# A decoder layer with retrieval over 16384 experts: the last block's scores from one dense product, with v rows gathered alone

## The reference

```python
q = (xb @ wq).reshape(PEER_BLOCK, PEER_HEADS, 2, PEER_HALF)        # 8 heads
s = jnp.einsum('thpd,hpkd->thpk', q, subkeys)                      # 128 keys a side
sv, si = lax.top_k(s, PEER_TOPK)                                   # 16
cand, cand_id = ...                                                # 16 x 16 pairs of a head
top_v, top_i = lax.top_k(cand, PEER_TOPK)
expert = jnp.take_along_axis(cand_id, top_i, axis=-1)              # 8 x 16 = 128 a token
gate = softmax(top_v)
act = gelu(einsum('thkd,td->thk', u_tab[expert], xb))              # 128 dots of width 1024
out = einsum('thk,thkd->td', gate * act, v_tab[expert])
```

## Time and profile before

| | |
|---|---|
| runs | 4586.57, 4585.86, 4565.0 us; median 4585.86 |
| profiled execution, span from first to last instruction | 4574.9 us (its own time is not listed; the runs stand 10 us below to 12 us above the span) |
| TensorE | 3277.9 us busy, 72% |
| VectorE | 2488.2 us, 54% |
| GpSimd | 1648.0 us, 36% |
| ScalarE | 801.6 us, 18% |
| DMA | 1400.14 MB, mean 306 GB/s |

### The profile page before, as it was taken

How to read it: one execution, slowest core, us unless ns; L and a number is a source line. 1 busy time by engine, 2 the same in 40 slices (tenths; PEclk the granted TensorE clock), 3 DMA queues, 4 the chain that set the end, 5 groups by cost and what they waited for, 6 DMA issues and landing times. The chain is left out here.

```text
span 4574.9 us, 46652 instructions
## 1 busy us (share of the span) xinstructions
PE 3277.9 (72%) x15679; PEld 1680.7 (37%) x15679; DVE 2488.2 (54%) x7735; ACT 801.6 (18%) x1284; POOL 1648.0 (36%) x1379
## 2 busy tenths in 40 slices
PE   8899997736389666686678676667666667666666
PEld 2798896636056441341145344124210101111110
DVE  2245553126764445577755454557786555555554
ACT  2232333232014113110013211211000100000000
POOL 1211104523245444442345444344333333333332
PEclk9999998968589886897789888678765666666666
DMA  7211103533789889898889898999899999999998
GB/s 278 73 58 49 39 29 131 171 118 111 274 334 407 338 354 379 345 384 341 337 348 405 345 393 356 383 375 362 354 387 360 415 404 405 409 412 409 414 411 346
DMA packets 243430, 1400.14 MB, mean 306 GB/s; under 512 B 30661, under 2 KB 47685, under 8 KB 100986
## 3 DMA queue, kind: packets, MB, share of 16 engines
q0 software_dynamic: 156672, 1140.92, 62.1%
q1 hardware_dynamic: 86522, 256.22, 15.5%
HBM read 1345.59 MB, written 51.43 MB: 305 GB/s over the span
## 5 line engine op out<-in xcount | busy, mean ns | idle before, releaser
L1057 DVE CUSTOM_DVE_ANT_0 peer_uv<-peer_uv,all_PS 128x512 f32<-128x512 f32 x2176 | 1435.3, 685 | 1164.2 <-DMA peer_uv<-in_uv,peer_idx 804.8
L996 PE MATMUL all_PS<-peer_hT,peer_sel 96*128 96x512 bf16 x2176 | 1002.4, 484 | 1027.4 <-DVE peer_halves L1057 842.5
L979 POOL DMA_INDIRECT peer_uv<-in_uv,peer_idx x1088 | 1043.4, 959 | 1756.9 <-PE all_PS L1015 1379.6
L996 PEld LDWEIGHTS all_PS<-peer_hT,peer_sel 96*128 96x128 bf16 x2176 | 203.0, 102 | 2002.9 <-DVE peer_halves L1057 1632.6
L1015 PE MATMUL all_PS<-peer_uv,peer_zw 128*32 128x512 f32 x4352 | 871.7, 849 | 2.4 <-DVE peer_zw L1077 2.4
L867 POOL TENSOR_TENSOR flow_w_lo<-flow_w,flow_w_hi 128x1024 fp32r<-128x1024 f32 (+1 forms) x204 | 460.4, 2261 | 456.5 <-ACT flow_w_hi L860 455.9
L1031 ACT ACTIVATE peer_ge<-peer_pre 128x4 f32<-128x4 f32 x272 | 55.7, 205 | 2109.7 <-DVE peer_pre L1063 2109.6
L887 PE MATMUL all_PS<-mix_h_hi,flow_w_hi 128*128 128x384 f32 (+1 forms) x672 | 279.6, 416 | 32.2 <-POOL flow_w_lo L867 31.8
L860 ACT ACTIVATE flow_w_hi<-flow_w 128x1024 fp32r<-128x1024 f32 (+1 forms) x204 | 203.5, 1003 | 359.2 <-PE all_PS L889 110.7
L888 PE MATMUL all_PS<-mix_h_lo,flow_w_hi 128*128 128x384 f32 (+1 forms) x672 | 226.3, 337 | 0.0
L889 PE MATMUL all_PS<-mix_h_hi,flow_w_lo 128*128 128x384 f32 (+1 forms) x672 | 226.1, 336 | 0.0
(11 more groups left out here) (290 smaller groups left out, 4670.4 us busy)
## 6 DMA issues: line engine op xcount, KB each, us to landing
cond_w<-in_w_ada SPq DMA_DIRECT2D x12, 2048.0 KB, 8.1
flow_w<-in_w_gate_ab SPq DMA_DIRECT2D x48, 512.0 KB, 7.1
flow_w<-in_w_query SPq DMA_DIRECT2D x48, 512.0 KB, 7.7
flow_w<-in_w_conv SPq DMA_DIRECT2D x36, 512.0 KB, 4.5
peer_uv<-in_uv,peer_idx POOLq DMA_INDIRECT x1088, 10.4
gla_w<-in_w_heads SPq DMA_DIRECT2D x24, 512.0 KB, 4.4
flow_w<-in_w_proj_b SPq DMA_DIRECT2D x24, 512.0 KB, 7.8
flow_w<-in_w_out SPq DMA_DIRECT2D x24, 512.0 KB, 8.4
```

Of the source, the lines that this page charges most:

```text
L979: self.nc.gpsimd.indirect_dma_start(out=self.uv[:, n % self.NUV, :], out_offset=None, in_=self.A["uv"], in_offset=bass.IndirectOffsetOnAxi ...
L996: nc.tensor.matmul(PS[:, f, :], self.sel[:, c:c + 1].broadcast_to([3 * GR, P]), self.hT[:, g % self.NH, f * 512:(f + 1) * 512], start=True ...
L1057: nc.vector.tensor_tensor_reduce(part, part, PS[:, f, :], 1.0, 0.0, ALU.mult, ALU.add, self.halves[:, d, f, e:e + 1]).then_inc(M["dotted"], 1)
```

## The change

The last block (part 2, tiles 6, 7 and 8 in order, 384 tokens, `SCORED`) is treated in another way than the rest.

- In part 2's pick stage TensorE multiplies the tile's h with the whole table u^T, in 32 chunks of 512 experts, each in four steps of two slices of k, with the same three products. The table's blocks (`u_chunks`, 128 of 512 KB) go through the weight stream, halves included. `emptied` copies each chunk of scores from PSUM to `line`, and SyncE stores it in DRAM (`scores2`). h_hi and h_lo of the keys stage now live through pick.
- For a scored token `fetch` issues two indirect DMAs: the v row of each expert (4 KB, from the same table seen as 32768 rows) and one element of 4 bytes for each expert from the stored scores. There is no `spread` and no `dots`; `gelu` reads the fetched scores. `gat.limit` keeps scored tokens from being fetched before the last stage.
- The ring of buffers is 18 slots of 4 KB a partition (a whole row takes two), `AHEAD` is 12 where slots are free, and the stream has four raw buffers in place of two.
- `SHARES` is given for each part. A part without scored tiles ends at its last share: part 0 at 24 and part 1 at 100. Part 2 ends at token 704.
- norm makes no `pieces` for scored tiles. `make_low_on_vector` is called in all stages and applies to blocks in `by_vector`, which is empty here, because only a part behind a scored one fills it.

```diff
+SCORED = frozenset((6, 7, 8))
+CHUNK, KPAIR = 512, 2
+NCHUNK, NKP = NK * NK // CHUNK, KD // KPAIR
...
-    def __init__(self, sc, sources, raws=2, pairs=4):
-        self.sources, self.raws, self.pairs = sources, raws, pairs
+    def __init__(self, sc, sources, by_vector, raws=4, pairs=4):
+        self.sources, self.by_vector, self.raws, self.pairs = sources, by_vector, raws, pairs
...
-    NUV, NZ, ND, NH, AHEAD = 10, 3, 4, 6, 4
+    NUV, NZ, ND, NH, NS, AHEAD = 9, 3, 4, 6, 8, 12
+    NIDX = 6
...
     def fetch(self, pool, upto):
 
-        for n in self.steps("pool", upto + self.AHEAD if upto else 0):
+        end = min(upto, self.limit)
+        while upto and end < min(upto + self.AHEAD, self.limit) and self.freed[end] <= max(upto - 3, 0) // BT:
+            end += 1
+        for n in self.steps("pool", end):
             u, c, j = self.tokens[n]
+            q, e = divmod(n, BT)
             if n == self.before[u]:
                 pool.wait_ge(self.M["idx_set"], u + 1)
-            if n >= self.NUV:
-                pool.wait_ge(self.M["v_mm"], (n - self.NUV) // BT + 1)
...
+            if self.freed[n]:
+                pool.wait_ge(self.M["v_mm"], self.freed[n])
+            at, slot = j * GR + c, self.place[n]
+            index = lambda of: bass.IndirectOffsetOnAxis(ap=of[:, u % self.NIDX, at:at + 1], axis=0)
+            if not self.scored[n]:
+                self.nc.gpsimd.indirect_dma_start(out=self.uv[:, slot:slot + 2, :].rearrange("p s d -> p (s d)"), out_offset=None,
+                                                  in_=self.A["uv"], in_offset=index(self.idx)).then_inc(self.uv_in[slot], 16)
+                continue
+            s = self.scored_before[q]
+            if e == 0 and s >= self.NS:
+                pool.wait_ge(self.M["gelled"], q - self.NS + 1)
+            self.nc.gpsimd.indirect_dma_start(out=self.uv[:, slot, :], out_offset=None,
+                                              in_=self.A["uv"].rearrange("e (s d) -> (e s) d", s=2), in_offset=index(self.idx)
+                                              ).then_inc(self.uv_in[slot], 16)
+            self.nc.gpsimd.indirect_dma_start(out=self.score[:, s % self.NS, e:e + 1], out_offset=None,
+                                              in_=self.A[f"scores{self.part_of[u]}"].rearrange("d p (s o) -> (d p s) o", o=1), in_offset=index(self.spot)
+                                              ).then_inc(self.s_in[s % self.NS], 16)
...
         @block.tensor
         def _(pe):
-            for j in range(NJ):
-                gat.spread(pe, upto(j))
-                i, q = divmod(j, PARTS_OF)
+            def chunk(j):
+
+                c, k2 = divmod(j, NKP)
+                u_hi, u_lo = (a[:, (w0 + j) % w.pairs].rearrange("p (k f) e -> p k (f e)", k=KPAIR) for a in (w.hi, w.lo))
+                pe.wait_ge(w.low, w0 + j + 1)
+                for i, t in enumerate(scored):
+                    m = c * nd + i
+                    tok = slice(part.at[t], part.at[t] + P)
+                    if k2 == 0 and m >= 3:
+                        pe.wait_ge(l_out, m - 2)
+                    for kk in range(KPAIR):
+                        k = KPAIR * k2 + kk
+                        nc.tensor.matmul(bank(m), h_hi[:, k, tok], u_hi[:, kk, :], start=(k == 0), stop=False)
+                        nc.tensor.matmul(bank(m), h_hi[:, k, tok], u_lo[:, kk, :], start=False, stop=False)
+                        last = nc.tensor.matmul(bank(m), h_lo[:, k, tok], u_hi[:, kk, :], start=False, stop=(k == KD - 1))
+                        if k == KD - 1 and i < nd - 1:
+                            last.then_inc(c_mm, 1)
+                        if kk == KPAIR - 1 and i == nd - 1:
+                            last.then_inc(w.used, 1)
+                        gat.spread(pe, turns.within(j, KPAIR * i + kk + 1, KPAIR * nd))
...
+            def emptied(c):
+
+                for i in range(nd):
+                    m = c * nd + i
+                    if i < nd - 1:
+                        act.wait_ge(c_mm, c * (nd - 1) + i + 1)
+                    else:
+                        act.wait_ge(w.used, w0 + c * NKP + NKP)
+                    if m >= NR:
+                        act.wait_ge(l_saved[m % NR], 16 * (m // NR))
+                    nc.scalar.activation(line[:, m % NR, :], bank(m), ACT.Copy).then_inc(l_out, 1)
             for j in range(NJ):
                 gat.gelu(act, upto(j))
-                i, q = divmod(j, PARTS_OF)
+                if nd:
+                    if j % NKP == NKP - 1:
+                        emptied(j // NKP)
+                    w.make_high(nc, act, w0 + j + w.pairs)
...
-SHARES = (94, 50, 38, 42, 90, 100)
+SHARES = {0: (0, 0, 0, 0, 0, 24), 1: (94, 50, 38, 42, 90, 100), 2: (86, 42, 38, 38, 60, 120)}
...
+                    shares = SHARES[part.index]
+                    end = gat.before[part.tiles[part.scored[0]]] if part.scored else shares[-1]
+                    marks = [lo + (end - lo) * sum(shares[:i]) // sum(shares) for i in range(len(shares) + 1)]
                     part.m_before = done
+                    gat.limit = min([gat.before[part.tiles[i]] for i in part.scored], default=T)
```

More of the change, by code:

```diff
@@ L958, in __init__ @@
         assert self.h_at == sorted(self.h_at)
+        self.rank = [0]
+        self.place, self.landed, self.freed = [], [], []
+        uses = [0] * (2 * self.NUV)
+        owner = {}
+        at = 0
+        for n, alone in enumerate(self.scored):
+            wide = 1 if alone else 2
+            slot = at % (2 * self.NUV)
+            assert slot + wide <= 2 * self.NUV
+            self.rank.append(self.rank[-1] + (not alone))
+            uses[slot] += 1
+            self.place.append(slot)
+            self.landed.append(16 * uses[slot])
+            had = [owner[slot + i] for i in range(wide) if slot + i in owner]
+            self.freed.append(max(had) // BT + 1 if had else 0)
+            for i in range(wide):
+                owner[slot + i] = n
+            at += wide
+        self.scored_before = [sum(self.scored[0:BT * q:BT]) for q in range(T // BT + 1)]
+        self.part_of = {u: part.index for part in PARTS for u in part.tiles}
         self.at = {e: 0 for e in ("pool", "pe", "act", "dve", "sp")}
-        self.loaded = 0
+        self.loaded, self.limit = 0, T
         self.ready_tiles = set()
@@ L1469, in norm_phase @@
         second = lambda i: m_rows[0:R[i], i, :]
+        ahead = lambda i: sum(d < i for d in part.dotted)
         turns = Turns(lo, hi, NJ)
@@ L1490, in _ @@
                 if stage == 2:
-                    for piece, (src, made) in enumerate(((first, one), (third, three), (fourth, four))):
-                        sp.wait_ge(made, i + 1)
+                    for piece, (src, made) in enumerate(((first, one), (third, three), (fourth, four)) if i in part.dotted else ()):
+                        sp.wait_ge(made, ahead(i) + 1)
                         sp.dma_start(A["pieces"][u, piece, 0:R[i], :], src[0:R[i], :]).then_inc(p_saved, 16)
@@ L1504, in _ @@
                 stage, i = divmod(j, nt)
[L1505 to L1507 removed]
+                if stage == 2 and i in part.dotted:
+                    pool.wait_ge(one, ahead(i) + 1)
+                    if ahead(i) == 0:
                         pool.wait_ge(x2_saved, 16 * nt)
                     nc.gpsimd.tensor_tensor(second(i), x[0:R[i], i, :], first[0:R[i], :], ALU.subtract).then_inc(two, 1)
[L1510 to L1511 removed]
+                    pool.wait_ge(three, ahead(i) + 1)
+                    pool.wait_ge(two, ahead(i) + 1)
                     nc.gpsimd.tensor_tensor(fourth[0:R[i], :], second(i), third[0:R[i], :], ALU.subtract).then_inc(four, 1)
@@ L1546, in _ @@
                     act.wait_ge(h2_done, i + 1)
-                    if i:
-                        act.wait_ge(p_saved, 48 * i)
-                        act.wait_ge(two, i)
-                    nc.scalar.activation(first[0:R[i], :], x[0:R[i], i, :], ACT.Copy).then_inc(one, 1)
+                    if i in part.dotted:
+                        if ahead(i):
+                            act.wait_ge(p_saved, 48 * ahead(i))
+                            act.wait_ge(two, ahead(i))
+                        nc.scalar.activation(first[0:R[i], :], x[0:R[i], i, :], ACT.Copy).then_inc(one, 1)
                     for e in range(2):
@@ L1557, in _ @@
                                              ACT.Copy).then_inc(t_out, 1)
-                    act.wait_ge(two, i + 1)
-                    nc.scalar.activation(third[0:R[i], :], second(i), ACT.Copy).then_inc(three, 1)
+                    if i in part.dotted:
+                        act.wait_ge(two, ahead(i) + 1)
+                        nc.scalar.activation(third[0:R[i], :], second(i), ACT.Copy).then_inc(three, 1)
         @block.vector
@@ L2104 @@
 _SCRATCH = {"ob": (NB, P, H, 2, MOST), "h1": (NB, P, KD, MOST), "rows": (NROW, NC, D), "sig": (NB, KD, P, 2, MOST),
```

(3 more changed lines are left out.)

188 lines of the change are left out of this document (137 added, 51 removed).

## The result

The changed kernel takes 4975.51 us (median of four runs, 4952.71 to 4979.99) against 4579.58 of before: a ratio of 1.086, interval 1.083 to 1.089. The forecast was 5093 us, in a range of 4760 to 5390, and slower with 0.93. The number and the sign hold, in part by luck: the experiments show that a cost that the sum did not have, the shorter ring of buffers, took some 77 us of the changed kernel, and that other terms were too large by more than that.

A forecast was written before the change was run, and what follows sets the result against it. The transfer of gathered rows was taken as the bound from 1252 us on, PE next. 1252 + 620 + 1320 + 910 + 980 gave 5082 us of span, so 5093 us with 11 more; range 4760 to 5390.

The forecast's parts named there:

- ahead and part 0: All up to part 0's end: part 0 left at 529 us, ending at 1252; extra raw buffers counted zero.
- part 1: Part 1, gathering 76 tokens instead of 296, becomes like part 0: 620 us, between 580 and 700, saving 425.
- part 2, four stages: Mix, merge, out with norm, and keys stay DMA-bound at present rates with more tokens: 1320 us against 983.
- pick with dense: Part 2's pick stage: PE needs 794 us, DMA some 760; imperfect packing makes it 910, against 261 before.
- last stage: 384 scored tokens paced by POOL's two issues, 2.49 us each: 980 us with the tail, against 1034.
- two reasons given: Last stage: an element fetch costs POOL a row gather's issue, from 144 packets each and 0.94 us busy at every issue.
- B: Last stage: the element fetch binds the DMA, 3.18 us a token, stage 1246, whole 5359 us; chance 0.14.
- E: Last stage: POOL's second issue is short, bytes bind, stage 517 us, whole given as 4520, not slower; chance 0.06.
- C: Stages pack well: part 2 takes 1960 us, part 1 600, whole 4803 us; chance 0.22.
- The estimate of 5209 us: Whole kernel if element fetches cost the skill's 10.5 ns for each of 144 packets, 2.79 us a scored token.
- The drain that I feared: Pick stage: each new chunk waits for ACT's drain, behind gelu of undotted tokens; no size of its own.
- The move of tokens: 220 full gathers go from part 1 into part 2: part 2 +986 us, dense product included, part 1 -425.

The follow-up runs named there:

- nofetch: The changed kernel with the element fetch of scores left out and the gelu reading a constant: 4529.1 us in a single run.
- s10r3: The changed kernel with ten ring rows, three raw weight buffers, three score-index slots, five h buffers and the table of ones freed after attention: 5028.06 us, 1.100.
- s10r2: The changed kernel with ten rows in the ring and two raw weight buffers: 4998.13 us, 1.092.
- c9r2: ctl (nine ring rows) with two raw weight buffers in place of four: 4808.52 us, 1.049.
- c10r2: ctl with ten rows in the ring in place of nine and two raw weight buffers in place of four: 4607.1 us, 1.007.
- moved: ctl with the new shares and part 1 ending at token 100 in place of 320, nothing scored: 4877.0 us, 1.067.
- ctl: The changed kernel with no tile scored and the shares and part ends of before; ring, lookahead and four raw buffers stay: 4773.65 us, 1.043.
- end320: The changed kernel with part 1 ending at token 320 as before, the rest as it is: 4957.72 us, 1.084.
- alone: The changed kernel with no token gathered during part 2's pick stage; tokens 515 to 703 go to the last stage: 5372.63 us.
- onepass: The changed kernel with two of the dense part's three products left out, 768 matmuls in place of 2304: 4912.66 us.

## Why the prediction was right, and where it was not

Step by step, in us of span, predicted and measured:

| step | predicted | measured | what the runs say |
|---|---|---|---|
| ahead and part 0 | 1252 | 1239 | raw buffers -22, a few us more ahead |
| part 1 | 620 | 573 | merge 73 for 93, keys 123 for 138: PE idle 9 and 22 us, not 26 and 28 |
| part 2, four stages | 1320 | 1387 | 1309 with ten rows |
| pick with dense | 910 | 793 | PE's own sum was 794 |
| last stage | 980 | 985 | POOL, 2.50 us a token |
| sum | 5082 | 4978 | |

The **last stage** was right in mechanism and size: 768 issues at 1.25 us, the stage 5 us off. POOL's own row of issues without a pause shows that they are the bound, and in nofetch half of them go and the stage is 548 us. Of the two reasons given, one was wrong: an element fetch does not make the 144 packets of a row fetch. nofetch moves 156672 packets through the gather's queue for 1088 issues, 144 each, and the changed kernel 168960, so the 384 element fetches make 12288, or 32 each. The other reason, 0.94 us at every issue whatever it moves, held: the element fetch takes 0.95 with a quarter of the packets. Rivals B and E fall: the fetch never bound the DMA (0.72 busy), and its issue was not short. Scores land 4.0 us after their issue (median), with gathers of rows beside them. C, the well-packed course, came true in the pick stage and in part 1 (573 us, under C's 600 and under the 580 that I had called the least), and not in part 2's first stages. The estimate of 5209 us from the Trainium skill, "DMA: Bandwidth & Descriptors", section "Bandwidth", took its 10.5 ns for each of 144 packets; there are 32, and POOL's pace decides before the DMA does. What one such packet takes, no run here shows.

The **pick stage** was right in what it is (PE's 794 us) and wrong by the 116 us that I put on top for two nearly equal resources that would not pack. They packed: PE was busy 95% of it. That 794 is so near the stage's 793 is luck all the same: both terms were too large. A matmul costs 0.228 us (at a granted 1.00), not the 0.243 scaled from a mix stage at 0.90, and a token (750 - 525) / 189 = 1.19 us of PE, not 1.24; PE's work was 750 us, and 43 us of idle time made it 793. The drain that I feared costs 13 us in all (PE waiting for the copied line).

**Part 2's four stages** were sized at the rates of before. With ten rows that is right to 11 us (1309 for 1320). One slip is in the 1320: merge was divided by 373 GB/s, the rate of the stages behind it; by its own 355 in the earlier trace rows it is 236 us and the sum 1331. With the nine that the change leaves, they take 77 or 78 us more (1387 against 1310 in s10r3 and 1309 in s10r2). That is the step that failed: the ring of buffers was in the diff, I told of it in the description and left it out of the sum. It costs 201 us where all stages are bound by gathers (c9r2 against c10r2), and 77 or 78 here, because part 1 has few gathers left, the pick stage is PE's, and the last stage's 18 slots of 4 KB are enough when POOL is the bound. My sum had no term for it and came out above the measured time only because the pick stage was 117 us and part 1 47 us too dear. The 11 us that I added for the runs over the span are not there either: the profiled run took 4979.99 us for a span of 4978.2.

**The move of tokens**: I booked +986 us in part 2 and -425 in part 1, with the move and the dense product in one sum. The runs give the move 103 us by itself (moved against ctl) and 18 under the dense product (changed against end320). Taken step by step in this order, the 396 us are: ring, lookahead and raw buffers +194 (ctl), scored path +184 (end320 against ctl), move +18. These are no prices of the parts by themselves, because the parts act on each other: with the move first and the scored path second, they cost 103 and 99 us (changed against moved), and in the changed kernel the ring costs 77 or 78 us and not 194.

## What to carry to other kernels

An indirect fetch of 128 pieces cost the issuing engine nearly the same here for 4 bytes (0.95 us) or 8 KB (0.94) a piece. Replacing half of a row by an element halves the bytes and doubles the issues, so count issues before bytes. In a stretch bound by gathers, buffers are bandwidth; price every buffer that a change takes or gives by transfers in flight (landing time over time per token), even if the change is about something else. And where two resources of nearly one size meet, start from the larger one: here the stage took 43 us more than PE's own work.

## What the runs showed of the hardware that I had not expected

- One row of ring, of ten: 411 to 376 GB/s in a stage that gathers 8 KB rows with a landing time near 10 us (ctl against c10r2), and 101 us in the last stage (c9r2 against c10r2).
- An indirect DMA of 128 elements of 4 bytes keeps GpSimd 0.95 us and the next one can start 1.25 us later; one of 128 rows of 4 or 8 KB, 0.94 and 1.24.
- PE's granted clock was 1.00 through 529 us of back-to-back matmuls (alone), 0.98 with gathers beside them, 0.79 with two thirds of them left out (onepass), and 0.58 in a last stage where it is busy for a third; in nofetch the same products, in 548 us in place of 985, ran at 0.97.
- The same last stage took 985 us in four kernels and 1101 to 1103 in two, with long gaps in TensorE's issue that no wait explains, and 116 to 124 us of waits of POOL behind them (in alone, too).
